# Two transformer blocks on one core: key tiles' scores merged by a masked copy, and the turns of a unit pair done together

## The reference

```
# block one: tokens are a grid of 8 rows x 64 columns; each query sees 16 columns x 8 rows = 128 keys
col_idx = jnp.clip(cols - 8, 0, 48)[:, None] + jnp.arange(16)
s = einsum('bqhd,bwqkhd->bhqwk', qr, kg) * scale + bias     # bias from rpb[h, row_rel, col_rel]
p = softmax(s over the 128 keys);  out = einsum('bhqwk,bwqkhd->bqhd', p, vg)

# block two: each query sees itself and the 127 tokens before it
dist = qi + BLOCK - kj;  band = (dist >= 0) & (dist < 128)  # keys: the tile before and the own tile
probs = softmax(concat([scores masked by band, sink]))[..., :-1];  out = probs @ v
```

## Time and profile before

| | us |
|---|---|
| median of 3 runs | 1208.78 (1207.12 to 1209.7) |
| span of the profiled execution | 1207.1 |
| PE busy in it | 1197.9 |
| DVE busy | 646.3 |
| ACT busy | 485.3 |
| POOL busy | 549.0 |

### The profile page before, as it was taken

The page is one execution under the profiler, slowest core; times in us unless marked ns, Lnnn a source line. Parts: engine busy times, 40 slices in busy tenths (PEclk is TensorE's granted clock), DMA queues, the critical chain, the costliest instruction groups (busy, mean ns, idle before and its releaser), DMA issues.

```text
span 1207.1 us, 16893 instructions
## 1 busy us (share of the span) xinstructions
PE 1197.9 (99%) x5700; PEld 984.0 (82%) x5700; DVE 646.3 (54%) x964; ACT 485.3 (40%) x731; POOL 549.0 (45%) x314
## 2 busy tenths in 40 slices
PE   9999999999999999999999999999999999999998
PEld 7777788888888888888777888888888888888888
DVE  5788765331243214484786355476677136632666
ACT  5455545432232213244565433344554224322444
POOL 4833144443444444464323666554355444444433
PEclk9999999999999999999999999999999999999999
DMA  8531133333332333233321333343233332333221
GB/s 199 153 96 54 36 114 96 99 92 103 89 104 87 105 90 93 73 111 106 86 62 35 97 99 97 108 131 99 78 104 105 103 89 87 104 105 88 88 69 70
DMA packets 220115, 114.76 MB, mean 95 GB/s; under 512 B 4171, under 2 KB 218913, under 8 KB 220065
## 3 DMA queue, kind: packets, MB, share of 16 engines
q1 hardware_dynamic: 219905, 113.83, 32.6%
q10 hardware_dynamic: 160, 0.27, 0.1%
HBM read 111.99 MB, written 2.10 MB: 95 GB/s over the span
## 4 chain that ended last, share of the span: by engine, by line
PE 94%; DVE 2%; SPq 1%; DMA 1%; issue 1%; ACT 0%; POOL 0%; ACTq 0%; DVEq 0%
PE ps L1434 87%; PE ps L1788 3%; PE ps L1596 1%; PE ps L1612 1%; PE ps L1586 1%; DMA w_stage<-in_w_in 1%; SPq L517 1%; SPq L504 0%; DVE mid L1086 0%; DVE sq_sum L943 0%; PE ps L1649 0%; DVE rms L1019 0%; SPq L479 0%; SPq L471 0%; POOL w_lo L573 0%
## 5 line engine op out<-in xcount | busy, mean ns | idle before, releaser
L573 POOL TENSOR_TENSOR w_lo<-w_stage,w_hi 128x1024 fp32r<-128x1024 f32 x216 | 527.5, 2448 | 630.7 <-ACT w_hi L657 630.7
L1434 PE MATMUL ps<-h_hi,w_hi 128*128 128x512 f32 x1100 | 432.3, 393 | 1.0 <-POOL w_lo L573 0.5
L1434 PE MATMUL ps<-h_hi,w_lo 128*128 128x512 f32 x1100 | 428.4, 389 | 0.0
L1434 PE MATMUL ps<-h_lo,w_hi 128*128 128x512 f32 x1100 | 428.2, 389 | 0.0
L657 ACT ACTIVATE w_hi<-w_stage 128x1024 fp32r<-128x1024 f32 x216 | 226.9, 1058 | 442.3 <-PE ps L1434 425.8
L1434 PEld LDWEIGHTS ps<-h_hi,w_hi 128*128 128x128 f32 x1100 | 206.5, 188 | 48.9 <-issue 4.4
L1434 PEld LDWEIGHTS ps<-h_hi,w_lo 128*128 128x128 f32 x1100 | 206.5, 188 | 43.4
L1434 PEld LDWEIGHTS ps<-h_lo,w_hi 128*128 128x128 f32 x1100 | 206.6, 188 | 42.1 <-issue 0.2
L936 DVE TENSOR_TENSOR mid<-ps,rs 128x512 f32<-128x512 f32 x130 | 88.5, 687 | 217.8 <-PE ps L1434 217.6
L1434 PE MATMUL ps<-g_hi,w_hi 128*128 128x512 f32 x496 | 193.7, 390 | 0.0
L1434 PE MATMUL ps<-g_hi,w_lo 128*128 128x512 f32 x496 | 193.0, 389 | 0.0
(11 more groups left out here) (190 smaller groups left out, 848.6 us busy)
## 6 DMA issues: line engine op xcount, KB each, us to landing
w_stage<-in_w_up SPq DMA_DIRECT2D x66, 512.0 KB, 3.8
w_stage<-in_w_in SPq DMA_DIRECT2D x48, 512.0 KB, 3.9
w_stage<-in_w_down SPq DMA_DIRECT2D x32, 512.0 KB, 3.6
w_stage<-in_w_gate SPq DMA_DIRECT2D x22, 512.0 KB, 3.8
w_stage<-in_w_out SPq DMA_DIRECT2D x16, 512.0 KB, 3.6
w_stage<-in_w_down SPq DMA_DIRECT2D x16, 384.0 KB, 3.1
mid<-in_x SPq DMA_DIRECT2D x4, 512.0 KB, 6.3
w_stage<-in_w_attn_branch SPq DMA_DIRECT2D x8, 256.0 KB, 2.7
```

Of the source, the lines that this page charges most:

```text
L573: pool.tensor_tensor(w_lo[:, s, c], w_stage[:, s, c], low_of(w_hi[:, s, c]), ALU.subtract).then_inc(w_lo_ready, 1)
L1434: ins = pe.matmul(bank(par if banks is None else banks, m), a, b, start=first and i == 0, stop=last and i == 2)
```

## The change

Scores are still computed for two key tiles. Then one predicated copy on DVE lays the seen scores of one key tile over those of the other, in PSUM, so that only 128 columns are left for a query tile instead of 256. Exponentials, sums and transposes work on 128 columns. After the transposes the values are split again into two key tiles by a product with 0/1 masks.

- `merged_scores` takes the place of `negated_scores`: `copy_predicated` on 2 x 128 columns, a wait for it, two custom instructions of 128 columns.
- The products with the inverse sums go from DVE to ACT (`normalise`, two of 128 columns); the reciprocal stays on DVE (`inverse_sums`).
- `turn_pair`: the 4 transposes of both units of a pair stand together (2 for each unit). They stand after the first of the stage's two parts of projection matmuls. DVE turns no unit any more.
- `copy_pt` on ACT goes; `split_turned` on DVE (512 columns from PSUM by a mask) takes its place, for both units of a pair, at the end of an odd unit.
- Block one: for query tile 0 each of the two value matmuls of a head takes 64 columns instead of 128. Block two: for query tile 0 the scores have 128 columns instead of 256.
- Tables: `bias` has 2 x 128 columns a head instead of 4 x 128, made by two selects, a copy and an addition on POOL; 0/1 masks `mask1`, one of them turned by PE and completed on DVE ahead of the first `qk_invert`; `mask2` anew.

```diff
-                    q = probs(p, u)[:, i * 256:(i + 1) * 256]
+                    q = probs(p, u)[:, i * P:(i + 1) * P]
                     act.activation(q, q, ACT.Exp, scale=-1.0, bias=neg_max[:, u % 2, i:i + 1],
                                    accum_out=exp_sum[:, u % 2, i:i + 1]).then_inc(exp_done, 1)
-            def copy_pt(u, pt):
...
+            def normalise(u, p):
+                act.wait_ge(inv_ready, u + 1)
+                for i in range(2):
+                    q = probs(p, u)[:, i * P:(i + 1) * P]
+                    ins = act.activation(q, q, ACT.Copy, scale=inv_sum[:, u % 2, i:i + 1])
+                ins.then_inc(probs_ready, 1)
...
+            def merged_scores(u, bs, p, tables, factor, bound):
+                own = ps[:, 4 + u % 2, :].rearrange("p (i s c) -> p i s c", i=2, s=2)
...
+                dve.copy_predicated(own[:, first:2, 1, :], taken, own[:, first:2, 0, :]).then_inc(scores_merged, 1)
+                dve.wait_ge(scores_merged, u + 1)
+                for i, table in enumerate(tables):
+                    ins = dve.tensor_tensor_reduce(
+                        out=probs(p, u)[:, i * P:(i + 1) * P], in0=own[:, i, 1, :],
+                        in1=table, scale=-factor, scalar=bound, op0=ALU.add, op1=ALU.min,
+                        accum_out=neg_max[:, u % 2, i:i + 1])
+                ins.then_inc(scores_read, 1)
+            def split_turned(u, pt, masks, apart):
+                dve.wait_ge(probs_turned, u // 2 * 2 + 2)
                 if u >= 2:
-                    dve.wait_ge(pv_done, u)
+                    dve.wait_ge(pv_done, u - 1)
...
+                    ALU.mult).then_inc(pt_ready, 1)
...
+            dve.tensor_copy(mask1[:, 2, :], ps[:, 5, 256:256 + P]).then_inc(mask1_turned, 1)
+            dve.wait_ge(mask1_turned, 1)
+            dve.tensor_scalar(mask1[:, 4, :], mask1[:, 2, :], -1.0, 1.0, ALU.mult, ALU.add).then_inc(mask1_ready, 1)
...
                 if u in SUMS_AT:
                     pool_sums(*SUMS_AT[u])
+                if 3 <= u < UNITS + 2 and u % 2:
+                    for v in (u - 3, u - 2):
+                        split_turned(v, pt1, mask1[:, 2:6, :].rearrange("p (s i) c -> p s i c", s=2), 0 in unit1(v)[1])
...
-            def turn_probs(u, p):
...
+            def turn_pair(u, p):
+                pe.wait_ge(probs_ready, u + 2)
+                pe.wait_ge(pt_ready, u)
+                for e in range(2):
+                    for i in range(2):
+                        ins = pe.transpose(ps[:, 6, e * 256 + i * P:e * 256 + (i + 1) * P],
+                                           probs(p, u + e)[:, i * P:(i + 1) * P], ident[:, :])
+                    ins.then_inc(probs_turned, 1)
...
-                if 4 <= u < UNITS + 2:
-                    turn_probs(u - 2, p1)
                 beside_unit(BESIDE1[u] if u < SPAN else [])
+                if 2 <= u < UNITS + 2:
+                    turn_pair(u - 2, p1)
```

More of the change, by code:

```diff
@@ L397, in probs @@
         def probs(p, u):
[L399 to L408, removed]
+            return p[:, u % 4, :]
         def unit1(u):
             return 2 * (u // 4) + u % 2, ((3, 0), (1, 2))[u // 2 % 2]
-        def keys1(b):
-            return (b - 1, b) if b else (0, 3)
         def unit2(u):
@@ L458, in by_chunk, with repeated @@
             return ap.rearrange("p (w j c) -> p j w c", j=4, c=16)
-        def twice(ap):
-            return bass.AP(ap.tensor, ap.offset, [list(ap.ap[0]), [0, 2], list(ap.ap[-1])])
+        earlier = mask1[:, 0:2, :].bitcast(mybir.dt.int32)
+        before = mask2[:, 2, :].bitcast(mybir.dt.int32)
+        def repeated(ap, count):
+            return bass.AP(ap.tensor, ap.offset, [list(ap.ap[0]), [0, count], list(ap.ap[-1])])
         block = ctx.enter_context(nc.Block())
@@ L594, in bias_tables @@
                 edges = bias_in[:, h, 8:8 + ROWS * CB].rearrange("p (w k) -> p w k", k=CB)[:, :, 0:16]
[L595 to L601, removed]
+                early, late = (t.rearrange("p (w k) -> p w k", k=16) for t in (bias[:, h, 0, :], bias_late[:, h, :]))
+                select(early, rows[:, :, 0:16], ROWS - 1, [[0, ROWS], [ROWS, 16]], -1, fill=0.0)
+                select(late[:, :, 0:15], rows[:, :, 16:31], -ROWS, [[0, ROWS], [-ROWS, 15]], 1,
+                       fill=0.0).then_inc(bias_parts, 1)
+                pool.tensor_copy(bias[:, h, 1, :].rearrange("p (w k) -> p w k", k=16), edges)
+                pool.wait_ge(bias_parts, h + 1)
+                pool.tensor_tensor(early[:, :, 0:15], early[:, :, 0:15], late[:, :, 0:15],
+                                   ALU.add).then_inc(bias_ready, 1)
             low_part(1, 1)
@@ L1067, in normalise @@
                 dve.reciprocal(inv_sum[:, i, :], total).then_inc(inv_ready, 1)
[L1068 to L1078, removed]
-                if u >= 2:
-                    dve.wait_ge(pv_done, u)
[L1081 to L1086, removed]
-                ins.then_inc(pt_ready, n)
@@ L1089, in negated_scores @@
-            def negated_scores(u, p, tables, factor, bound):
-                for i, table in enumerate(tables):
-                    c = slice(i * 256, (i + 1) * 256)
-                    ins = dve.tensor_tensor_reduce(
-                        out=probs(p, u)[:, c], in0=ps[:, 4 + u % 2, c], in1=table, scale=-factor,
-                        scalar=bound, op0=ALU.add, op1=ALU.min, accum_out=neg_max[:, u % 2, i:i + 1])
-                ins.then_inc(scores_read, 1)
+            def merged_scores(u, bs, p, tables, factor, bound):
+                own = ps[:, 4 + u % 2, :].rearrange("p (i s c) -> p i s c", i=2, s=2)
+                first = 1 if u >= UNITS and bs[0] == 0 else 0
+                if u >= UNITS:
+                    taken = repeated(before, 2 - first)
+                elif 0 in bs:
+                    taken = earlier
+                else:
+                    taken = repeated(earlier[:, 0, :], 2)
+                dve.copy_predicated(own[:, first:2, 1, :], taken, own[:, first:2, 0, :]).then_inc(scores_merged, 1)
[6 more added lines that the diff above has]
+                ins.then_inc(scores_read, 1)
@@ L1344, in _ @@
                         take_in(n, m, n, (cb[:, 2 * half + m, :], cc[:, 2 * half + m, :], cx[:, m, :])[part])
+                if 3 <= u < UNITS + 2 and u % 2:
+                    for v in (g - 3, g - 2):
+                        split_turned(v, pt2, mask2[:, 3:5, :].rearrange("p (s i) c -> p s i c", i=1), False)
             def take_branches(n, par):
```

154 lines of the change are left out of this document (85 added, 69 removed).

## The result

The changed kernel takes 1224.23 us (median of 4, 1224.02 to 1228.91) against 1208.76 of the kernel before in the same job: a ratio of 1.0143, interval 1.0131 to 1.0155. The prediction had the sign right and the size wrong: +15.5 us where it said +4.4, 6.7 above the end of its range. The profiled execution is the longest of the four (span 1227.2; the others 1222.3 to 1222.6), so its span is 20.1 above that of before, and its rows account for that larger number, not for the 15.5.

A forecast was written before the change was run, and what follows sets the result against it. PE was taken to bound the kernel (busy 1197.9 of 1207.1 us). Waits of 10.8 us less a gain of 6.4 made +4.4 on 1208.8, rounded to 1213 us, range 1204.5 to 1217.5.

The forecast's parts named there:

- term (1): PE's wait before 48.8 in block one, behind DVE's mask complement: +0.45 us, up to +2.4 if POOL holds it.
- term (5): PE's waits in block two: splits in stages 4, 6, 8 (3.1), turns in stages 2 (0.5) and 16 (0.3): +3.9 us.
- The gain: What PE saves in the two attentions: turns 5.2, scores 0.8, values 0.4, together 6.4 us.
- the turns: PE's transposes in both blocks, one group a pair between matmuls: 0.40 us saved a pair, 5.2 in all.
- the halved scores: Score matmuls in 4 stages of block two, half of them with half the columns: 0.2 us saved a stage, 0.8 in all.
- The values of block one: Value matmuls in 4 stages, eight of sixteen with half the columns: 0.1 us saved a stage, 0.4 in all.
- the column formula: Pricing block one's value matmuls by columns: up to 0.26 us a stage, 1.0 in all; the prediction took less.
- the reading of the load row: Block one's values: a weight load of 136 ns, as long as a pair's step, stays, so only 0.1 us a stage.
- terms (2) to (5): PE's waits: block one stages 6 and 8 +0.5, stage 10 2.2, stage 14 +3.75; block two +3.9 us.
- rival C: Predicated copy on DVE costs 0.9 us instead of 0.45, or POOL holds the splits: +4, 1217 us; chance 0.12.
- Rival A and B: A: stages' waits don't add up, 1205.5 us, chance 0.20. B: half the waits are hidden, 1208.9 us, chance 0.17.

The follow-up runs named there:

- m_psum: The changed kernel with the mask's complement made from PSUM, where the turned mask lies, not from its SBUF copy: 1218.98 us, ratio 1.009.
- all3: Changed kernel, mask complement from PSUM, splits earlier on DVE, second unit's reciprocal and normalisation in its own turn: 1205.32 us, ratio 0.9976 to the kernel before.
- best: all3 with the splits of pair 12 one unit earlier and the pooling sums there behind unit 15: median 1203.73 us, ratio 0.9967 to the kernel before.
- b_scalar: The kernel before plus one unused SBUF-to-SBUF product of 128 columns on DVE, where the changed kernel makes its mask's complement: 1218.56 us, ratio 1.0093.
- b_late: The kernel before plus one SBUF-to-SBUF product of 128 columns on DVE at 65.95 us: 1208.37 us, ratio 1.0001.
- s_early: The changed kernel with a pair's two splits earlier in DVE's turn, in both blocks: 1218.67 us, ratio 1.0083 to the kernel before.
- m_inv: m_psum with the second unit's reciprocal and normalisation moved into its own turn, splits not moved: 1224.8 us, ratio 1.0132 to the kernel before.
- both: The changed kernel with the edits of s_early and m_psum together: 1211.43 us, ratio 1.0032 to the kernel before.

## Why the prediction was wrong

In short: the waits that term (1) and term (5) should have held were larger than they said, and the sum had no term for the clock. Term (1) is the largest single miss, but even without it (m_psum, +11.5 us) the time would have lain above the range.

**The gain: right in kind, somewhat too small.** In block two, stage 6 of the trace before begins at 607.55 and stage 8 at 616.21. In all3, where nothing waits there:

```profile
599.29 0.93 PE L1775 MATMUL ps<-mid 64*128 64x128 f32 x8
...
607.10 1.13 PE L1775 MATMUL ps<-mid 64*128 64x256 f32 x8
...
615.32 0.93 PE L1775 MATMUL ps<-mid 64*128 64x128 f32 x8
```

Stage 6 lasts 8.22 instead of 8.66, so the turns gave 0.44 a pair (predicted 0.40). Stage 4, with the halved scores, lasts 7.81 instead of 8.43: another 0.2, as predicted. The values of block one gave 0.2 a stage, not 0.1: they take 0.82 (112.37 to 113.19 in the changed kernel) instead of 1.03. There the column formula was right, and the reading of the load row, which the prediction backed with the Trainium skill's view of narrow matmuls, was wrong; it was worth 0.4 us. With 0.44 for each of 14 pairs less 0.44 for the new turn, 0.8 for scores and 0.8 for values that is 7.3, against 6.4 predicted (an estimate: the stages named stand for the others). PE's busy time agrees: in best, where no clock falls, it is 7.4 below that of before (1190.5 and 1197.9). In the changed kernel it fell by 1.4 only, because matmuls at the lower clock take longer.

**The new waits, terms (2) to (5): right where they were named.** m_psum is the fair test, since nothing came before them.

```profile
91.62 1.09 PE L1623 MATMUL ps<-mid 128*64 128x128 f32 x16 [0.19 <-DVE mid L1099]
...
107.75 0.50 PE L1517 MATMUL ps<-g_hi,head_rows 32*128 32x512 f32 x2 [0.52 <-DVE neg_max L1086]
...
114.68 1.09 PE L1623 MATMUL ps<-mid 128*64 128x128 f32 x16 [2.19 <-DVE mid L1099]
...
135.59 1.15 PE L1623 MATMUL ps<-mid 128*64 128x128 f32 x16 [2.61 <-DVE mid L1099]
137.88 1.12 PE L1597 MATMUL ps<-ident,mid 128*128 128x128 f32 x4 [1.14 <-ACT mid L748]
```

Predicted and found, in that order: stages 6 and 8 of block one, +0.5 and +0.3 (0.52 instead of 0.20; the 0.19 at 91.6 takes the place of 0.21 at 79.96 before); stage 10, 2.2 and 2.19; stage 14, 2.5 and 2.61 for the values and 1.25 and 1.14 for the turn; block two, stages 4, 6 and 8, 1.1, 0.9, 1.1 and 1.12, 0.92, 1.12; the turn of stage 2, 0.5 and 0.62. The masked copy took 423 ns at 256 columns (predicted 0.42), so rival C had no ground.

**Term (5) was incomplete.** It held that in later stages of block two the splits are in time. In the changed kernel stages 12, 16 and 18 waited 0.38, 2.09 and 0.62 = 3.1 us; the wait of 0.3 for a turn that it gave stage 16 did not come. DVE in front of the longest:

```profile
668.25 1.54 DVE L1318 SCALAR_TENSOR_TENSOR mid<-mid,vec 128x512 f32<-128x512 f32 x2
669.71 0.68 DVE L940 TENSOR_TENSOR mid<-ps,rs 128x512 f32<-128x512 f32 x1
670.31 1.27 DVE L1099 TENSOR_TENSOR mid<-ps,mask 128x512 f32<-128x512 f32 x2
```

The prediction counted the evacuation (L940) ahead of the splits, but not the convolution stages (L1318), and in stage 16 PE has no scores ahead of its values, so it asks 1.06 earlier. In block one it gave stage 16 no wait; that was 0.4 to 0.5.

**Term (1) failed.** It took +0.45, with +2.4 as the most, "if POOL holds the product". Measured: a wait of 7.83 in place of 0.53, so +7.3. The 2.4 was the length of one POOL product. But POOL's products come in pairs there (42.80, 4.76 for two, in the trace before), and the late product L1027 was held again. The pair could be read in the trace before. The second hold could not: the next pair begins at 52.90 there, and a product made four us late would have ended just ahead of it, so its 3.5 us are in part chance. m_psum shows that the operand's place is the cause, b_scalar that the product alone does it without the rest of the change, b_late that it doesn't do so at another place, with one POOL product near its end. (The Trainium skill, SBUF — State Buffer, SBUF: two separate sides, says that POOL and certain DVE operations lock each other out for one whole instruction. The trace agrees that the one stands while the other works, but the hold outlasted an instruction: 42.49 to 46.34 takes in the end of the first product of the pair and all of the second.)

**The clock was not in the sum.** The prediction made no term of it. In m_psum the windows 100 to 120, 120 to 140 and 140 to 160 stand at 0.91, 0.91 and 0.92; on working matmuls that is a loss of 4.5 us, in the changed kernel 6.6.

The two sums by what the traces show, over the span of before: m_psum, waits 14.5 - 0.9 = 13.6, clock 4.5, gain -7.3, together 10.8, measured 10.9. The changed kernel, waits 21.4 - 0.9 = 20.5, clock 6.6, gain -7.3, together 19.8, measured 20.1. Without the hold, the forecast of +4.4 would still have met +11.5: 3.5 of unlisted waits in block two and in stage 16 of block one, 4.5 of clock, less 0.9 of gain that was under-counted, make 7.1 of which none was in the sum. Rival A and B said that waits would not add up; they do, and cost more than their sum.

What stays open: what ends a hold. In the changed kernel it ended 0.4 us after a POOL pair while POOL went on with selections, in s_early 1.7 us after one (44.53 and 46.20), and in b_scalar the product and the transpose behind it ended only with POOL's next product. It was not tried which of POOL's operations lets DVE in. Open too is what decides whether the clock falls behind a wait of 1.8 to 2.3 us (below).

## What to carry to other kernels

When PE has no slack, a change that puts DVE's work between two PE steps is priced by DVE's order in each stage, and the repair is order: the same arithmetic gave 1.0143, and 0.9967 with four moves on DVE and ACT and one operand read from PSUM. Put what PE waits for ahead of what it doesn't (splits before evacuations, convolution and pooling), and move a step that waits on another engine behind it, not in front. Price an SBUF-to-SBUF product that falls beside a run of POOL's by the whole run and by what it makes late, or read its operand from PSUM if it lies there, and add a clock term to PE's longer waits: in these traces every one of 2.6 us and more had one, and four of nine from 1.8 to 2.3.

## What the runs showed of the hardware

- A one-input product of 128 columns, SBUF to SBUF, took 0.46 us at the end of a POOL product, 3.70 and 3.85 where it began inside a POOL pair, and 10.78 in b_scalar, until the end of the product after the pair; from PSUM 0.29 beside a pair.
- PE's clock fell during or behind every wait of 2.61 us and more (2.61, 2.78, 4.12, 4.21, 4.29, 4.45, 7.83, 10.54) and behind none of 1.57 and less; the wait of 1.9 before PE's first matmul is left out. Between these it fell behind 1.82, 2.16, 2.19 and 2.20 and not behind 2.09, 2.11, 2.19, 2.25 and 2.29 (m_inv has five of these nine), so the length of the wait alone doesn't decide it there. The stretches at the lower clock lasted from 3.4 to some 10 us, the long ones in part while PE still waited.
- A masked copy PSUM to PSUM takes 423 ns for 256 columns and 290 for 128.
- s_early, with the hold, ran from 1211.06 to 1220.65 us in six executions, where `both`, the same without it, ran from 1211.08 to 1212.42. That the hold is what makes the time scatter isn't shown.
